# Attention scores in three fp32r products of split q and k, and the projections of a unit in the order k, q, v

## The reference

```python
def layer(i, h, ple, cache):
    u = rms_norm(h, g_mix_pre[i])
    qa, ka, va, qb, kb, vb = split_projection(u, w_in[i])
    ...
    oa = mixer_a_prompt(qa, ka, va, rel_bias[i])                  # 8 heads of 64, biased by relative distance
    ob = mixer_b_prompt(qb, kb, vb, lam, lam0, diff_subln[i])     # 8 heads, two softmax maps of 64 each
    ...
    g_a, g_b = jnp.split(jax.nn.sigmoid(u @ w_gate[i]), 2, axis=-1)
    mix = (g_a * (oa @ w_branch_a[i]) + g_b * (ob @ w_branch_b[i])) @ w_out[i]
    h = h + rms_norm(mix, g_mix_post[i])
    f = jnp.square(jax.nn.relu(rms_norm(h, g_ffn_pre[i]) @ w_up[i])) @ w_down[i]
    h = h + rms_norm(f, g_ffn_post[i])
    h = h + jax.nn.sigmoid(h @ w_ple_gate[i]) * rms_norm(ple @ w_ple[i], g_ple[i])
    return h, new

def diff_attention(q, k, v, q_pos, k_pos, lam, lam0, sub_g):
    s = jnp.einsum('bqhcd,bkhcd->bhcqk', q, k).astype(jnp.float32) * (HEAD_DIM ** -0.5)
    s = s - alibi_slopes(B_HEADS)[:, None, None, None] * dist
    p = jax.nn.softmax(jnp.where(valid, s, MASK_VALUE), axis=-1)
    a = (p[:, :, 0] - lam * p[:, :, 1]).astype(v.dtype)
    o = jnp.einsum('bhqk,bkhe->bqhe', a, v)
    o = rms_norm(o, sub_g) * (1.0 - lam0)
    return o.reshape(o.shape[0], o.shape[1], B_V_WIDTH)
```

## Time and profile before

| | |
|---|---|
| median of three runs | 1160.73 us |
| profiled execution, its own time | 1158.91 us |
| its span | 1156.2 us |
| TensorE (PE) busy | 1126.2 us, 97% |
| DVE, ACT, POOL busy | 490.7, 427.0, 509.0 us (42, 37, 44%) |
| DMA | 98.82 MB, 85 GB/s |

### The profile page before, as it was taken

One profiled execution on the slowest core, in us unless ns is written; L12 is line 12 of the kernel. 1 busy time (PEld: TensorE's weight loads), 2 busy tenths in 40 slices (PEclk: granted clock), 3 DMA queues, 4 the chain that ended last, 5 costly groups with the idle time before them and its releaser, 6 DMA issues.

```text
span 1156.2 us, 23228 instructions
## 1 busy us (share of the span) xinstructions
PE 1126.2 (97%) x8376; PEld 1072.2 (93%) x8376; DVE 490.7 (42%) x950; ACT 427.0 (37%) x923; POOL 509.0 (44%) x420
## 2 busy tenths in 40 slices
PE   8999999999799999999999899999999999999898
PEld 7888889888688889999999899999999999999897
DVE  5655555555444541112532567115313511442655
ACT  6444444454354443231223353122212222232352
POOL 3446455444343433443446554444434443444651
PEclk9999999999899999999999899999999999999999
DMA  6234423232133322232222212322222222222122
GB/s 179 84 94 120 115 85 89 72 102 82 58 94 94 93 68 78 83 102 77 82 82 82 64 56 81 91 82 82 82 82 82 82 82 82 81 82 85 52 74 82
DMA packets 167370, 98.82 MB, mean 85 GB/s; under 512 B 8833, under 2 KB 162682, under 8 KB 167314
## 3 DMA queue, kind: packets, MB, share of 16 engines
q1 hardware_dynamic: 159570, 82.05, 24.7%
q0 software_dynamic: 7744, 16.02, 4.5%
HBM read 88.57 MB, written 11.02 MB: 86 GB/s over the span
## 4 chain that ended last, share of the span: by engine, by line
PE 92%; DVE 6%; ACT 1%; DMA 1%; issue 0%; SPq 0%; ACTq 0%; DVEq 0%
PE proj L1333 77%; PE score L1452 3%; PE turn_out L1515 2%; PE turn_out L1545 2%; PE turn_out L1537 1%; PE turn_out L1484 1%; DVE wide L1199 1%; PE turn_out L1542 1%; PE score L1459 1%; DMA x_tm<-x_sample 1%; DVE hT L1228 1%; DVE act_lo L1217 1%; DVE act_lo L1221 1%; DVE act_lo L957 0%; PE score L1359 0%
## 5 line engine op out<-in xcount | busy, mean ns | idle before, releaser
L476 POOL TENSOR_TENSOR w_lo<-w_raw,w_hi 128x512 fp32r<-128x512 f32 x292 | 396.3, 1360 | 546.4 <-ACT w_hi L631 546.3
L1333 PE MATMUL proj<-act_hi,w_hi 128*128 128x288 f32 x1568 | 348.7, 304 | 6.8 <-DVE act_lo L1221 3.4
L1333 PE MATMUL proj<-act_hi,w_lo 128*128 128x288 f32 x1568 | 337.1, 297 | 0.0
L1333 PE MATMUL proj<-act_lo,w_hi 128*128 128x288 f32 x1568 | 337.0, 297 | 0.0
L631 ACT ACTIVATE w_hi<-w_raw 128x512 fp32r<-128x512 f32 x292 | 182.6, 629 | 403.3 <-PE proj L1333 403.2
L1333 PEld LDWEIGHTS proj<-act_hi,w_hi 128*128 128x128 f32 x1568 | 251.6, 190 | 18.9 <-issue 8.7
L1333 PEld LDWEIGHTS proj<-act_lo,w_hi 128*128 128x128 f32 x1568 | 253.9, 190 | 0.0
L1333 PEld LDWEIGHTS proj<-act_hi,w_lo 128*128 128x128 f32 x1568 | 253.8, 190 | 0.0
L1333 PE MATMUL proj<-mid_hi,w_hi 128*128 128x288 f32 x640 | 137.4, 295 | 0.0
L1333 PE MATMUL proj<-mid_lo,w_hi 128*128 128x288 f32 x640 | 137.3, 295 | 0.0
L1333 PE MATMUL proj<-mid_hi,w_lo 128*128 128x288 f32 x640 | 137.2, 295 | 0.0
(11 more groups left out here) (213 smaller groups left out, 1174.1 us busy)
## 6 DMA issues: line engine op xcount, KB each, us to landing
w_raw<-w_in SPq DMA_DIRECT2D x72, 256.0 KB, 2.9
w_raw<-w_up SPq DMA_DIRECT2D x64, 256.0 KB, 2.7
w_raw<-w_down SPq DMA_DIRECT2D x64, 256.0 KB, 2.8
w_raw<-w_gate SPq DMA_DIRECT2D x32, 256.0 KB, 2.7
w_raw<-w_branch_b SPq DMA_DIRECT2D x16, 256.0 KB, 2.7
w_raw<-w_out SPq DMA_DIRECT2D x16, 256.0 KB, 2.8
w_raw<-w_ple_gate SPq DMA_DIRECT2D x16, 256.0 KB, 2.8
out<-k_tm POOLq DMA_DIRECT2D x12, 256.0 KB, 2.8
```

The costliest lines, as they stand in the source:

```text
L476: pool.tensor_tensor(w_lo[:, slot], w_raw[:, slot], w_hi[:, slot].bitcast(F32), ALU.subtract).then_inc(lo_done, 1)
L1333: last = pe.matmul(out[:, h], w[:, slot, at], x[:, k, HALF * h:HALF * h + HALF], start=(k == 0 and s == 0), stop=(k == blocks - 1 and s == 2))
```

## The change

q and k are kept as a high part in fp32r and a low part, and so are the cached keys. The scores are then three products: hi·hi, lo·hi and hi·lo. The three projections of a unit come in the order k, q, v. ACT makes the high parts of k and q (`hi_of_kq`) and POOL the low parts (`lo_of_kq`) at k steps 9 and 17, DVE fills the two padded q (`pad_q`) at step 21; ACT writes `ckT_hi`, and DVE `ckT_lo`, which now frees `turn`. v has one buffer where it had two. Several tiles get other places in SBUF.

```diff
-            a_cols = (2 * AW, AW, 0)
-            b_cols = (3 * AW + 2 * NB * P, 3 * AW + NB * P, 3 * AW)
+            a_cols = (AW, 0, 2 * AW)
+            b_cols = (3 * AW + NB * P, 3 * AW, 3 * AW + 2 * NB * P)
...
+            def lo_of_kq(u, n, par):
+
+                at_least(pool, kq_hi, u * 2 + (n + 1))
+                raw, hi, lo = ((kT[par], k_hi[par], k_lo[par]), (q_raw, q_hi[par], q_lo[par]))[n]
+                pool.tensor_tensor(lo[:, :], raw[:, :], hi[:, :].bitcast(F32), ALU.subtract).then_inc(kq_split, 1)
...
+                    elif name == "k" and arg in (9, 17) and next_kind:
+                        lo_of_kq(u + 1, arg // 8 - 1, 1 - par)
...
+            def hi_of_kq(u, n, par):
+
+                job = u * 3 + (PJ_IN + n)
+                b = job.mod(2)
+                at_least(act, proj_free[b], (job + (-b)).over(2) + 1)
+                raw, hi = ((kT[par], k_hi[par]), (q_raw, q_hi[par]))[n]
+                act.activation(hi[:, :], raw[:, :], ACT.Copy).then_inc(kq_hi, 1)
...
-                        act.activation(ckT[:, :], turn[:, 0:SEQ], ACT.Copy).then_inc(turn_free, 1)
+                        act.activation(ckT_hi[:, :], turn[:, 0:SEQ], ACT.Copy).then_inc(ck_hi, 1)
...
-                dst = (vT, kT, qT)[n][par][:, :]
-                if n < 2 or gates:
-                    dve.tensor_tensor(halves(dst), acc[b], halves(x_row[:, :]), ALU.mult).then_inc(proj_free[b], 1)
-                else:
+                dst = (kT[par], q_raw, vT)[n][:, :]
+                if n == 1 and not gates:
+                    at_least(dve, kq_split, u * 2)
                     dve.scalar_tensor_tensor(out=halves(dst), in0=acc[b], scalar=0.125, in1=halves(x_row[:, :]),
                                              op0=ALU.mult, op1=ALU.mult).then_inc(proj_free[b], 1)
-                    at_least(dve, proj_free[b], (u * 3 + (PJ_IN + n - b)).over(2) + 1)
-                    dve.tensor_copy(q_pad[par][0:64, 0:SMP], dst[0:64, SEQ:T])
-                    dve.tensor_copy(q_pad[par][64:P, SMP:2 * SMP], dst[64:P, SEQ:T]).then_inc(q_padded, 1)
+                else:
+                    dve.tensor_tensor(halves(dst), acc[b], halves(x_row[:, :]), ALU.mult).then_inc(proj_free[b], 1)
+
+            def pad_q(u):
+
+                par = u.mod(2)
+                at_least(dve, kq_split, u * 2 + 2)
+                for pad, q in ((q_pad_hi[par], q_hi[par]), (q_pad_lo[par], q_lo[par])):
+                    dve.tensor_copy(pad[0:64, 0:SMP], q[0:64, SEQ:T].bitcast(F32))
+                    last = dve.tensor_copy(pad[64:P, SMP:2 * SMP], q[64:P, SEQ:T].bitcast(F32))
+                last.then_inc(q_padded, 1)
...
+                    elif name == "k" and arg == 21 and u.const != NU - 1:
+                        pad_q(u + 1)
+                    elif name == "CK":
+                        at_least(dve, ck_hi, u + 1)
+                        dve.tensor_tensor(ckT_lo[:, :], turn[:, 0:SEQ], ckT_hi[:, :].bitcast(F32), ALU.subtract
+                                          ).then_inc(turn_free, 1)
...
+                def scores(i):
+                    n = keys(i)
+
+                    for m in range(2):
+                        at_least_alone(pe, biased, u * JOBS + (2 * i + m - 1 if i else 0))
+                    for s, (q, k) in enumerate(((q_hi, k_hi), (q_lo, k_hi), (q_hi, k_lo))):
+                        for m in range(2):
+                            h = slice(64 * m, 64 * m + 64)
+                            last = pe.matmul(score[:, 512 * m:512 * m + n], q[par][h, P * i:P * i + P], k[par][h, 0:n],
+                                             start=(s == 0), stop=(s == 2))
+                            if s == 2:
+                                last.then_inc(scored, 1)
...
+                    for s, (q, c, k) in enumerate(((q_pad_hi, ckT_hi, k_hi), (q_pad_lo, ckT_hi, k_hi),
+                                                   (q_pad_hi, ckT_lo, k_lo))):
+                        pe.matmul(score[:, 0:SEQ], q[par][:, :], c[:, :], start=(s == 0), stop=(s == 2))
+                        last = pe.matmul(score[:, SEQ:T], q[par][:, :], k[par][:, SEQ:T], start=(s == 0), stop=(s == 2))
+                    last.then_inc(scored, 1)
...
-                            for n in (1, 2):
-                                job = u * 3 + (PJ_IN + n)
-                                b = job.mod(2)
-                                at_least(pe, proj_free[b], (job + (-b)).over(2) + 1)
+                            at_least(pe, kq_split, u * 2 + 2)
...
+                        if name == "V4":
+                            job = u * 3 + (PJ_IN + 2)
+                            b = job.mod(2)
+                            at_least(pe, proj_free[b], (job + (-b)).over(2) + 1)
```

More of the change, by code:

```diff
@@ L208, in encoder_layer @@
             lam_s = sb("lam_s", [P, 4], F32, start)
-            dist_i = sb("dist_i", [P, TW], I32, start)
-            dist = sb("dist", [P, TW], F32, start)
             band_sb = sb("band_sb", [2 * NA, BW], F32, start)
-            idle_w, idle_x = sb("idle_w", [P, P], F32R, start), sb("idle_x", [P, 512], F32R, start)
         mid_hi, mid_lo = sb("mid_hi", [P, NB, T], F32R), sb("mid_lo", [P, NB, T], F32R)
+        with ExitStack() as band_only:
+            sb("oa_hi_first", [P, T], F32, band_only)
+            tab_b = [sb(f"tab_b{b}", [P, TW], F32, band_only) for b in range(2)]
+            o_sq = sb("o_sq", [P, 2, P], F32, band_only)
+            sb("oa_lo_first", [P, NA * T - 2 * TW - 2 * P], F32, band_only)
+            o_tm = [sb(f"o_tm{b}", [P, QB, P], F32, band_only) for b in range(2)]
         with ExitStack() as branch_a:
@@ L217, in encoder_layer @@
             with ExitStack() as att:
[L220 to L223, removed]
+                kT = [sb("kT0", [P, T], F32, att)]
+                q_raw, vT = sb("q_raw", [P, T], F32, att), sb("vT", [P, T], F32, att)
+                kT.append(sb("kT1", [P, T], F32, att))
+                k_hi, k_lo, q_hi, q_lo = ([sb(f"{name}{b}", [P, T], F32R, att) for b in range(2)]
+                                          for name in ("k_hi", "k_lo", "q_hi", "q_lo"))
                 k_tm, v_tm = sb("k_tm", [P, QB, P], F32, att), sb("v_tm", [P, QB, P], F32, att)
-                ck, cv, ckT = (sb(n, [P, SEQ], F32, att) for n in ("ck", "cv", "ckT"))
+                ck, cv = (sb(n, [P, SEQ], F32, att) for n in ("ck", "cv"))
+                ckT_hi, ckT_lo = (sb(n, [P, SEQ], F32R, att) for n in ("ckT_hi", "ckT_lo"))
                 tab_a = [sb(f"tab_a{b}", [P, 2, TW], F32, att) for b in range(2)]
-                tab_b = [sb(f"tab_b{b}", [P, TW], F32, att) for b in range(2)]
+                with ExitStack() as early:
+                    dist_i, dist = sb("dist_i", [P, TW], I32, early), sb("dist", [P, TW], F32, early)
+                    idle_w, idle_x = sb("idle_w", [P, P], F32R, early), sb("idle_x", [P, 512], F32R, early)
                 prob = [[sb(f"prob{b}{m}", [P, T], F32, att) for m in range(2)] for b in range(2)]
@@ L669, in _ @@
             hi_part(Count(RING + 1))
+            def hi_of_kq(u, n, par):
[4 more added lines that the diff above has]
+                act.activation(hi[:, :], raw[:, :], ACT.Copy).then_inc(kq_hi, 1)
+            for n in range(2):
+                hi_of_kq(Count(0), n, 0)
             act.wait_ge(lam_ready, 1)
@@ L1491, in unit @@
                     elif name == "Tail":
[L1492 removed]
+                        last = pe.transpose(turn[0:SMP, 0:P], vT[:, SEQ:T], ident[:, :])
                         last = pe.transpose(turn[0:SMP, P:2 * P], kT[par][:, SEQ:T], ident[:, :])
```

35 lines of the change are left out of this document (16 added, 19 removed).

## The result

| | before | after |
|---|---|---|
| median | 1160.53 us (4 runs, 1159.56 to 1162.0) | 1193.38 us (4 runs, 1192.58 to 1195.8) |
| ratio | | 1.0289, interval 1.0274 to 1.0304 |
| span of the profiled execution, mean granted clock | 1156.2 us, 0.990 | 1191.0 us, 0.974 |

A forecast was written before the change was run, and what follows sets the result against it. TensorE, busy throughout each loop unit, was taken as the bound, with a chain of no room ahead of V4. Terms -5.0 + 10.8 + 5.6 + 1.5 + 0.7 + 3.4 = +17.0 us gave a median of 1177, range 1158 to 1188.

The forecast's parts named there:

- products: Scores and sample on TensorE: three fp32r products stream less than four fp32 passes, -0.42 us a unit, -5.0 us for twelve.
- loop boundaries: Ends of loop units: late q_lo, held pads and ckT_lo bring V4 2.7 us late at four boundaries, +10.8 us.
- outside the loop: Ends of units 0, 1, 6 and 7: V4 1.4 us late at each, +5.6 us.
- start: Start of unit 0: q_lo behind two w_lo and k_lo, then pads, v and ckT_lo, delay V4, +1.5 us.
- between A units: Three boundaries between A units: ckT_lo shows a little ahead of V4, 0.25 us each, +0.7 us.
- clock: TensorE's lower granted clock after V4's new waits: +3.4 us, bounds 0 and 12.
- With four new waits of 2.7 I take every second one as followed by it: Loop boundaries: half of V4's four new waits followed by 1.7 us lost at the lower clock, +3.4 us.
- my worse rival: N on DVE in A units also held up by POOL, or the clock drops after every wait: 1186 us, chance 0.1.
- So the first pad waits for the first w_lo, the second for the second: Pad copies on DVE at a loop unit's end: each ends 0.05 behind its w_lo, pads end at 199.1, not 197.77.
- the sample's term: Sample product on TensorE: three fp32r products take 0.83 us instead of 1.03, -0.20 us a unit.
- the pads do not wait at all: Rival: pads on DVE, now casts, are not held by POOL; -2.6 us, 1158 us, chance 0.2.
- the signs that I named: V4 waiting about 2.5 us, two pads over 1 us, v out 3.5 us after k23, loop units 33 to 34, S3 0.9.

The follow-up runs named there:

- the filled run: The change plus 20 extra matmuls, results unused, just ahead of V4's wait for turn in units 2 to 8: 1181.09 us, ratio 1.0185.
- the run in which POOL waits: The change plus a wait on POOL: the w_lo of step 19 comes only when the next unit's padded q is written: 1164.17 us, ratio 1.0039.
- the grouped run: The change with q's split at step 16 (B units: ACT's part behind T (3, 0)), sample products of 512 columns together, then those of 64: 1154.86 us.

## Why the prediction was wrong

The direction, the place and the chain were right: V4 is late by q_lo, the held pads, v and ckT_lo. The sum, term by term, in us:

| term | forecast | measured | from |
|---|---|---|---|
| products | -5.0 | -3.8 | 12 x (0.05 - 0.09 - 0.12 - 0.16 + 0), the scores' rows |
| loop boundaries | +10.8 | +14.0 | V4's waits of 3.53, 3.75, 3.49, 3.21 |
| outside the loop | +5.6 | +8.1 | 0.92 + 2.27 + 2.98 + 4.55, less 2.66 before |
| start | +1.5 | +2.2 | first V4 at 44.53, before 42.29 |
| between A units | +0.7 | 0 | 31.93 a unit, no wait |
| clock | +3.4 | +14.0 | 296.31 - 282.35, the filled run |
| sum | +17.0 | +34.5 | span +34.8 |

**The step that failed most** is "With four new waits of 2.7 I take every second one as followed by it". At all seven boundaries whose wait was 2.27 us or more the clock went to the lower level (1.2 GHz) around the end of the wait: the mean clock of those units was 0.91 to 0.95, in the first A unit 0.86. The price of one fall was too small as well. I had taken 3.4 us at the lower level; three of the seven lasted 3.4, the other four 6.8. One of each:

```profile
147.00:150.41 3.41, 3.41 (x15) 3.03 (x13) 1.42 (x7) 2.00 (x6) 0.53 (x1) 0.50 0.00 0
181.13:187.96 6.83, 5.48 (x25) 4.57 (x25) 2.62 (x12) 3.60 (x11) 2.15 (x2) 0.50 0.08 31
```

The filled run measures what this cost: 14.0 us, where 3.4 was forecast. The upper bound that I named, 12, was nearer than what I took, and my worse rival (1186) still lay below the result; the range was too narrow on the side that the mechanism itself pointed to.

**The second** is "So the first pad waits for the first w_lo, the second for the second". In the loop and at the end of unit 1 the first waits for both, 2.47 to 2.79. At the ends of units 6 and 7 it waits through the issue of the cv DMA as well, which ends at 288.95 in unit 6:

```profile
285.79 3.15 DVE L1028 CAST q_pad_hi<-q_hi 64x64 fp32r<-64x64 f32 x1 [4.26 <-POOL q_lo L519]
```

At the end of unit 0, where the second w_lo was not ready in time (POOL idle for 0.28), the first pad waited for one of them, 1.25. Why the two engines take turns at the program's start (1.26 and 1.25 beside two w_lo, in the profile after too) and not in the loop is not shown.

**The third**, the products: the pair of half-array matmuls was measured well (S3 0.90 against 0.93), but the sample's term of -0.20 a unit was wrong, since 0.0175 was taken, from the four records of the fp32 product, for each of its six matmuls, where each pair of 512 and 64 columns takes 0.10 more than its columns. By the rule that I weighed against the term (the Trainium skill, TensorE: Matmul & The Clock Gate, LDWEIGHTS; an estimate of 107 ns for a load of 128 columns) S0 to S2 would have been at 0.85, which no row shows. At the sample's products the steps of 0.11 behind 64 columns in the grouped run agree with it.

Of the rivals, "the pads do not wait at all" falls with the 2.47, and the cast does behave as a copy there. What it would have cost is shown by the run in which POOL waits: 1164, in which the w_lo that it moved still cost V4 1.1 us in each loop unit.

**The order k, q, v** stood at nothing in the prediction. Alone it is worth -3.5 us, since it takes the two pad copies out of the chain ahead of V4; with the change the late pads are back in that chain, so nothing of it is left.

Of the signs that I named, S3 came as said (0.90); v is taken out 4.6 us behind k23 in the loop (3.5 was said), and the loop's units take 36.4 to 37.3 us (33 to 34).

The change's idea was not what cost: with the split of q moved ahead of Tail's DMAs, and its high part behind ACT's copy for T (3, 0), the same products give -5.5 us, of which the order alone brings -3.5. The 2 us between the two medians are little more than their intervals (1.2 and 1.5 us either way); the loop's three stretches show the products' part more clearly (93.37 against 94.79).

## What to carry to other kernels

A small DVE instruction in a chain with no room is priced by what GpSimd runs beside it, not by its size: 0.19 us or 2.5 to 3.2 us for the same 64 columns. Before adding one, find what GpSimd does at that moment and behind it, its DMA issues too, and move either of the two by a step; here one step was worth more than 30 us. And idle waits of TensorE of 2.3 to 4.6 us had a second price, here another 14 us on 24 us of waits, in the matmuls that follow them; in the run without ckT_lo three waits of 2.3 to 2.8 had none, so this price is best measured by filling the wait.

## What the runs showed of the hardware that was not expected

- The hold is not one of copies: tensor_tensor with both inputs in SBUF was held through both w_lo (2.73 us for two of 64 columns), scalar_tensor_tensor likewise (1.12 instead of 0.34), and ckT_lo took up to 2.24 instead of 0.69 when its input from PSUM came from SBUF too. Taking v or q out, one input in PSUM, stayed at 0.76 beside any of them. The Trainium skill (SBUF — State Buffer, Who interferes with whom) says that a DVE instruction with two SBUF inputs contends with a GpSimd instruction that reads SBUF, and one with at most one does not, outside the modes that take both ports; the 2.73, 1.12 and 2.24 on the one side and the 0.76 on the other agree.
- Beside the issue of a DMA on POOL (0.80 us) a pad was sometimes held and sometimes not, as a cast and as a tensor_tensor. A cast was held to the end of the issue at the end of unit 1 (104.91 to 105.38) and ran in 0.19 in the loop (140.55); a tensor_tensor took 0.76 beside one (75.93) and 0.22 beside another (143.76). What decides it is not shown.
- One fall of TensorE's clock lasted 3.4 or 6.8 us here, and the waits that it came with were 1.54 to 4.55 us long; waits of 2.25 to 2.77 came without one.
